# Two expert stages rewritten as units of two column tiles, in a two-layer diffusion backbone

## The reference, cut to what matters

```python
scores = sigmoid(t @ router_w); sel = scores + router_bias      # t: (T, 1024), T = 512 or 256
idx = top_8_of_64(sel, limited to the best 4 of 8 groups)
w = scores[idx] / sum(scores[idx]) * 2.5
for e in range(64):                                             # w_gate, w_up: 1024 x 256, w_down: 256 x 1024
    rows = tokens that chose e
    y[rows] += ((silu(t[rows] @ w_gate[e]) * (t[rows] @ w_up[e])) @ w_down[e]) * w[rows, e]
out = y + swiglu(t, shared_w_gate, shared_w_up, shared_w_down)
```

## Time and profile before

| | us |
|---|---|
| median of three executions | 2116.54 |
| the profiled execution | 2115.48 |
| its span, from the first to the last instruction | 2113.5 |
| TensorE busy | 1841.8 (87%) |
| VectorE busy | 1147.1 (54%) |
| ScalarE busy | 751.6 (36%) |
| GpSimd busy | 323.1 (15%) |
| layer 0's expert matmuls, first to last | 468.2 to 1153.2 |
| layer 1's expert matmuls, first to last down product | 1573.3 to 2091.2 |

### The profile page before, as it was taken

One profiled execution on the slowest core, in us unless ns is written; L12 is line 12 of the kernel. 1 busy time (PEld: TensorE's weight loads), 2 busy tenths in 40 slices (PEclk: granted clock), 3 DMA queues, 4 the chain that ended last, 5 costly groups with the idle time before them and its releaser, 6 DMA issues. The chain is left out here.

```text
span 2113.5 us, 32804 instructions
## 1 busy us (share of the span) xinstructions
PE 1841.8 (87%) x9706; PEld 1177.2 (56%) x9707; DVE 1147.1 (54%) x1988; ACT 751.6 (36%) x1200; POOL 323.1 (15%) x365
## 2 busy tenths in 40 slices
PE   2798989769999999999998679973769999999996
PEld 0677864436667766666665268311435555555553
DVE  1424643267777777777775655464333343343344
ACT  1214431126666665656553134772101111111111
POOL 1210000011112111222221070120001111111110
PEclk9999989789999999999999889985879999999998
DMA  6761043518899999999994853633449999999993
GB/s 263 250 241 41 1 147 129 195 50 301 345 364 359 353 352 359 371 364 357 351 354 181 345 131 102 214 118 140 159 166 414 420 419 416 413 419 415 415 418 131
DMA packets 127189, 580.28 MB, mean 275 GB/s; under 512 B 31347, under 2 KB 52457, under 8 KB 66849
## 3 DMA queue, kind: packets, MB, share of 16 engines
q1 hardware_dynamic: 94624, 500.76, 60.8%
q0 software_dynamic: 32368, 76.74, 10.1%
q10 hardware_dynamic: 144, 2.10, 0.3%
HBM read 587.79 MB, written 38.90 MB: 297 GB/s over the span
## 5 line engine op out<-in xcount | busy, mean ns | idle before, releaser
L1497 DVE TENSOR_TENSOR m_w_lo<-mods,m_w_hi 128x1024 fp32r<-128x1024 f32 x264 | 311.6, 1222 | 33.1 <-ACT m_w_hi L1416 30.7
L1416 ACT ACTIVATE m_w_hi<-mods 128x1024 fp32r<-128x1024 f32 x264 | 263.9, 1049 | 21.5 <-PEq L1008 11.9
L1694 PE MATMUL ps<-m_wgu,m_xT 128*64 128x256 f32 x2112 | 251.1, 385 | 4.3 <-DVE m_xT L1793 4.3
L1368 PE MATMUL ps<-m_w_hi,m_x_hi 128*128 128x512 f32 x528 | 245.3, 465 | 5.6 <-DVE m_x_lo L1489 5.6
L1352 PE MATMUL ps<-m_wd,m_hidT 128*128 128x512 f32 x528 | 248.1, 592 | 0.9 <-DVE h L1505 0.9
L1694 PEld LDWEIGHTS ps<-m_wgu,m_xT 128*64 128x64 f32 x2112 | 159.1, 138 | 98.1 <-issue 46.9
L1368 PE MATMUL ps<-m_w_lo,m_x_hi 128*128 128x512 f32 x528 | 208.2, 394 | 0.0
L1368 PE MATMUL ps<-m_w_hi,m_x_lo 128*128 128x512 f32 x528 | 207.0, 392 | 0.0
L1799 DVE TENSOR_TENSOR h<-h,ps 128x512 f32<-128x512 f32 x132 | 90.5, 686 | 124.5 <-PE ps L1683 123.5
L1352 PEld LDWEIGHTS ps<-m_wd,m_hidT 128*128 128x128 f32 x528 | 95.5, 191 | 70.8 <-issue 63.6
L1284 POOL DMA_INDIRECT h<-h_rows,m_gidx x69 | 79.7, 1156 | 350.6 <-DVE m_gidx L1481 345.8
(11 more groups left out here) (316 smaller groups left out, 3173.0 us busy)
## 6 DMA issues: line engine op xcount, KB each, us to landing
m_wd<-in_moe_w_down SPq DMA_DIRECT2D x132, 1024.0 KB, 9.0
mods<-in_moe_w_gate SPq DMA_DIRECT2D x66, 1024.0 KB
mods<-in_moe_w_up SPq DMA_DIRECT2D x66, 1024.0 KB
m_wgu<-in_moe_w_gate SPq DMA_DIRECT2D x66, 1024.0 KB
m_wgu<-in_moe_w_up SPq DMA_DIRECT2D x66, 1024.0 KB, 12.7
c_rows<-y_rows SPq DMA_DIRECT2D x8, 2048.0 KB, 15.4
mods<-in_ada_w POOLq DMA_DIRECT2D x11, 1024.0 KB, 6.4
mods<-in_ada_w SPq DMA_DIRECT2D x11, 1024.0 KB, 4.8
```

Source lines behind the costliest of these rows:

```text
L1368: last = pe.matmul(g.ps[0:S, GU, :].rearrange("p (a f) -> p a f", a=2), x[:, q, k, :], w[:, q, :, k, :], start=(k == 0 and n == 0), stop=( ...
L1416: act.activation(w_hi[:, q, :, k, :], wgu[:, q, :, k, :], ACT.Copy).then_inc(hi_s, 1)
L1497: dve.tensor_tensor(w_lo[:, q, :, k, :], wgu[:, q, :, k, :], w_hi[:, q, :, k, :].bitcast(F32), ALU.subtract).then_inc(lo_s, 1)
L1694: last = pe.matmul(g.ps[half[s], GU, a * FE:(a + 1) * FE], xT[:, k, half[s]], wgu[:, q, s, a, k, :], start=(k == 0), stop=(k == KD - 1))
```

## The change

Both expert phases are replaced by one, `unit_phase`, and both weight classes by `UnitWeights`. An expert's rows are cut into halves of up to 64 rows. Two halves of the same expert make a *twin* unit, and what is left over after that (one half at most for each expert) is joined with another expert's into a *pair* unit. A twin unit loads its expert's weights once and uses them on both column tiles; a pair unit loads two experts. `side` is 1 for a pair and 0 for a twin. Pairs stand at even positions and twins at odd ones as long as there are both. By the counts above, layer 0 has 20 pairs (one with an empty second half) and 26 twins, 46 units; layer 1 has 32 pairs (one with an empty second half) and one twin, 33 units.

The step of a unit is that of the pair phase before. In layer 0 the `put` and `add` parts are left out; the result is copied to `ysb` and scattered, as before. In layer 0 the down weights have two buffers (in `g.mods`), in layer 1 one.

The weights of the second half come from GpSimd's queue, by an indirect transfer with one row of 8 KB for each partition. Where there is no second expert, the indices are out of bounds and nothing is moved. `routes.second` holds the indices; VectorE copies a unit's column to `gu_row` and `down_row` in each step. The first loads wait until the owners of the units are known (`known`), since the order of the experts now comes from the routing. The route phase computes the order in a longer chain of small VectorE operations, with TensorE's shared gate and up products placed around it. The calls of `recycle_semaphores` move ahead of `combine_phase`.

```diff
+HB = P // 2
+NU = 72
+SKIP = 65536.0
+def lead_of(layer):
+    return 2 if layer == 0 else 1
...
+class UnitWeights:
+    def __init__(self, g, sb, layer, routes, wd):
...
+        self.wgu = sb(tag + "wgu", [P, 2, 2, 2, KD, FE])
+        self.wd, self.depth = wd, wd.shape[1]
...
+    def gate(self, sp, e, q):
+        sp.dma_start(self.wgu[:, q, 0, 0, :, :], self.first_rows[0][bass.ds(e, 1)].rearrange("o p k f -> p (o k) f")).then_inc(self.gate_in[q], 16)
...
+    def _second(self, pool, dst, n, row, landed):
+        rows = self.second_rows[n]
+        pool.indirect_dma_start(dst, None, rows, bass.IndirectOffsetOnAxis(ap=row[:, 0:1], axis=0),
+                                bounds_check=rows.shape[0] - 1, oob_is_err=False).then_inc(landed, 16)
+    def gate2(self, pool, q):
+        self._second(pool, self.wgu[:, q, 1, 0, :, :].rearrange("p k f -> p (k f)"), 0, self.gu_row[q], self.gate2_in[q])
...
     def prefetch(self, sp):
-        for q in range(2):
-            for s in range(2):
-                self.gate(sp, 2 * q + s, q, s)
...
+        for u in range(2):
+            e = self.owner(sp, u, 0)
+            self.gate(sp, e, u)
+            self.up(sp, e, u)
+            if u == 0:
+                self.down(sp, e, u)
+    def prefetch2(self, pool):
+        for u in range(2):
+            pool.wait_ge(self.gu_row_s, u + 1)
+            self.gate2(pool, u)
+            self.up2(pool, u)
...
 def route_phase(g, layer, tiles, routes, weights):
...
                 sp.wait_ge(g.h_stored, 16 * g.h_stores)
+                sp.wait_ge(known, 3)
                 weights.prefetch(sp)
+            @block.gpsimd
+            def _(pool):
+                weights.prefetch2(pool)
...
+                shared_gate_up(0)
                 pe.wait_ge(masks, 1)
...
+                pe.wait_ge(parts_s, 1)
+                for n in range(2):
+                    pe.matmul(g.ps[:, RANKS, n * (E + 1):(n + 1) * (E + 1)], parts[:, n:n + 1].to_broadcast([E, P]), g.field("before_e", E),
+                              start=True, stop=True)
...
+                shared_gate_up(1)
+                pe.wait_ge(at_s, 1)
+                pe.wait_ge(number_s, 1)
+                pe.matmul(g.ps[:, OWN, 0:3 * NU], number[:, 0:1].to_broadcast([E, P]), at[:].rearrange("e s u -> e (s u)"),
+                          start=True, stop=True).then_inc(owners, 1)
+                for t in range(2, tiles):
+                    shared_gate_up(t)
...
-def expert_phase(g, layer, tiles, routes, weights):
-def expert_pair_phase(g, layer, tiles, routes, weights, total):
+def unit_phase(g, layer, tiles, routes, weights, total=None):
...
+    half = (slice(HB, P), slice(0, HB))
...
             def _(sp):
+                def load(i, q):
+                    e = weights.owner(sp, i, 0)
+                    sp.wait_ge(gate_done, i - 1)
+                    sp.sem_inc(issue, 1)
+                    weights.gate(sp, e, q)
+                    sp.wait_ge(up_done, i - 1)
+                    sp.sem_inc(issue, 1)
+                    weights.up(sp, e, q)
+                def load_down(i, d):
+                    e = weights.owner(sp, i, 0)
+                    sp.wait_ge(y_done, i - depth + 1)
+                    sp.sem_inc(issue, 1)
+                    weights.down(sp, e, d)
...
             def _(pool):
...
+                def step(i, q, r):
+                    pool.wait_ge(weights.gu_row_s, i + 3)
+                    pool.sem_inc(issue, 1)
+                    weights.gate2(pool, q)
+                    weights.up2(pool, q)
+                    gather(i + 2)
+                    pool.wait_ge(y_done, i + 1)
+                    pool.sem_inc(issue, 1)
+                    if depth == 1:
+                        weights.down2(pool, 1 - q, 0)
+                    else:
+                        pool.wait_ge(weights.down_row_s, i + 3)
+                        pool.sem_inc(issue, 1)
+                        weights.down2(pool, q, q)
+                    if total is None:
+                        scatter(i, q)
...
             def _(pe):
...
+                def project(q, r, side, a, loaded, loaded2, done, inside=None):
+                    pe.wait_ge(loaded[q], 16 * r + 16)
+                    pe.wait_ge(loaded2[q], 16 * r + 16)
...
                         for s in range(2):
-                            last = pe.matmul(g.ps[half[s], GU, a * FE:(a + 1) * FE], xT[:, k, half[s]], wgu[:, q, s, a, k, :],
+                            w = wgu[:, q, 0, a, k, :] if s == 0 else wgu[:, q, bass.ds(side, 1), a, k, :].rearrange("p o f -> p (o f)")
+                            last = pe.matmul(g.ps[half[s], GU, a * FE:(a + 1) * FE], xT[:, k, half[s]], w,
                                              start=(k == 0), stop=(k == KD - 1))
...
                 def step(i, q, r):
+                    side = pe.value_load(routes.side[0:1, bass.ds(i, 1)], min_val=0, max_val=1)
...
+                    if total is None or first(i):
+                        project(q, r, side, 1, weights.up_in, weights.up2_in, up_done)
                     else:
                         put(i - 1, 0, TB)
+                        project(q, r, side, 1, weights.up_in, weights.up2_in, up_done, inside=lambda: put(i - 1, 1, TB))
                     turn_tokens(i + 1)
...
             def _(dve):
...
                     dve.scalar_tensor_tensor(hid[:], act_g[:], meta[:, bass.ds(i, 1), GAIN], g.ps[:, GU, FE:2 * FE], ALU.mult, ALU.mult).then_inc(hid_s, 1)
+                    dve.tensor_scalar(weights.gu_row[q][:], routes.second[:, bass.ds(i + 2, 1)], 0.0, None, ALU.add).then_inc(weights.gu_row_s, 1)
                     tokens(i + 1)
...
-                expert_phase(g, 0, TILES, routes, weights)
+                unit_phase(g, 0, TILES, routes, weights)
+            g.recycle_semaphores()
             combine_phase(g, 0, TILES)
...
-                expert_pair_phase(g, 1, LAT_TILES, routes, weights, total)
+                unit_phase(g, 1, LAT_TILES, routes, weights, total)
```

More of the change, by code:

```diff
@@ L961, in route_phase @@
     tag = f"r{layer}"
-    E, S = EXPERTS, slots_of(tiles)
-    full = tiles * P // S
+    E = EXPERTS
+    full = tiles * P // HB
+    twin = full // 2
     with ExitStack() as st:
@@ L1148, in _ @@
                 dve.tensor_copy(chosen_bf[:], chosen[:]).then_inc(masks, 1)
-                for t in range(tiles):
+                dve.wait_ge(pos_done, 1)
+                chain.link(dve.tensor_copy(filled[:], g.ps[0:E, OWN, COUNT:COUNT + 1]))
+                chain.link(dve.tensor_scalar(over[:], g.field("iota_b", E)[:, 0:full], float(HB), filled[:, 0:1], ALU.mult, ALU.is_lt))
+                chain.done(dve.tensor_reduce(parts[:, 0:1], over[:, 0::2], AX.X, ALU.add))
+                chain.link(dve.tensor_reduce(parts[:, 1:2], over[:, 1::2], AX.X, ALU.add))
@@ L1150, in _ @@
+                chain.link(dve.tensor_tensor(firsts[:, 0:1], firsts[:, 1:2], all_two, ALU.add))
+                chain.link(dve.tensor_scalar(routes.count[:], firsts[0:1, 0:1], float(-1 - lead_of(layer)), None, ALU.add))
+                for t in range(1, tiles):
                     hidden(t)
-                dve.wait_ge(pos_done, 1)
-                for j in range(1, full):
-                    chain.link(dve.tensor_scalar(over[:, j:j + 1], g.ps[0:E, POS, COUNT:COUNT + 1], float(S * j), None, ALU.is_gt))
@@ new lines, in _ @@
+                for j in range(2, twin):
+                    chain.link(dve.scalar_tensor_tensor(turn, pos, float(P * j), turn, ALU.is_ge, ALU.add))
+                chain.link(dve.tensor_tensor(turn, turn, per_expert(two), ALU.add))
+                chain.link(dve.tensor_scalar(turn, turn, 1.0, firsts[:, 1:2], ALU.add, ALU.min))
+                chain.link(dve.tensor_tensor(base, per_expert(single[:]), turn, ALU.subtract))
+                chain.link(dve.tensor_tensor(base, base, alone, ALU.mult))
@@ L1653, in slots @@
                 def slots(i):
-                    experts = [owner(pe, 2 * i + s) for s in range(2)]
+                    experts = [weights.owner(pe, i, s) for s in range(2)]
                     pe.wait_ge(onehot_s, i + 1)
-                    if not peeled(i):
+                    if not first(i):
                         pe.wait_ge(idx_s, i)
```

769 lines of the change are left out of this document (265 added, 504 removed).

## The result

The changed kernel takes 2206.39 us (median of four runs, 2204.97 to 2218.56), the kernel before 2116.38 beside it: a ratio of 1.0443, with a 95% interval of 1.0403 to 1.0483. The forecast was 2084, so the sign was wrong, and so was the range. The profiled execution has a span of 2204.8 us, 91.3 more than before.

A forecast was written before the change was run, and what follows sets the result against it. TensorE was taken to bind layer 0, TensorE and DMA level in layer 1. The sum 2115.5 − 43 + 1 + 1 + 8 = 2082.5 us, 2084 against the median; the forecast's own range 2065 to 2105, overall 2045 to 2128.

The forecast's parts named there:

- TensorE's 13.2 us for a unit: Layer 0: TensorE needs 13.2 us a unit, 607 us for 46 units, as the stage's floor against 684.9.
- The DMA's 28.6 us for a period: Layer 0: a pair and a twin need 28.6 us of DMA, TensorE 26.4, so DMA binds; stage 642 us.
- the stage's −43: Layer 0's expert stage: 642 us, 43 less than before.
- The gather comes late in layer 0: Rival, chance 0.14: gather behind gate2 and up2 lands 4 to 5 us late; stage 690 to 730, time 2132 to 2172.
- q1 has nothing queued in parts of the period: Layer 0: argument against the late-gather rival, since gate and up loads are issued early.
- The two covers in layer 1: Layer 1 step: gather lands near 19 us, wanted at 24.3; down2 near 24.5, wanted at 27.5; both hold.
- +8: Layer 1's stage: 33 steps 0.3 us longer each, 10 us, less 2 for six loads spared.
- Two full queues are slower than one: Rival, chance 0.14: layer 1 falls to 383 GB/s, 17.1 us a step, 46 us instead of 8; time 2122.
- Where layer 0 starts: Route phase before layer 0: longer ordering against gathered rows needing no splitting, net +1 us.
- +6: Layer 0's route phase: VectorE's added links, longer slot chain and TensorE's wait for ranks push the tail 6 us.
- Between the layers +1: Layer 1's route phase: taken as 1 us longer.
- Register work: Register addresses of second-half matmuls: counted as hidden; as a rival, chance 0.08, 30 us in layer 1, 2114 or less.

The follow-up runs named there:

- the rows decoupled: Two buffers of gathered rows, gather ordered one unit earlier, in layer 0 or both layers; alone in layer 0 of the changed kernel 2107.74 us, in both 2113.94 us.
- two buffers alone: Changed kernel with two buffers of gathered rows and the gather one unit earlier in layer 0, nothing else: 2107.74 us, ratio 0.996.
- q0 at a third of the DMA: Kernel with two buffers of gathered rows in both layers, layer 1's down2 alone moved to SyncE's queue: 2066.78 us.
- the filler: Changed kernel with five 128x512 matmuls into an unused bank ahead of the wait for rows, every second unit of layer 0: 2222.59 us.

## Why the prediction was wrong, by its own steps

**TensorE's 13.2 us for a unit: right.** 13.12 in the rows above, 13.1 to 13.2 in the last six units, and 610.1 for the stage when nothing has to be loaded for the second half.

**The DMA's 28.6 us for a period, and 642 for layer 0: too dear, and not what was at work.** With the rows decoupled the period is 27.3 us and the stage 622 to 624 in four kernels. The error is 19 us, in the kernel's favour. Its likely source, which no run separates, is the price of a row, which came from a stage in which TensorE bound. What failed lies elsewhere: the sum took a period as the longer of the DMA's 28.6 and TensorE's 26.4 us, as if the two overlapped in full, and put no wait between them. The period measured is 32.8, and the stage's −43 was +42.1.

**"The gather comes late in layer 0" was a rival with 0.14, and is what happened.** Its mechanism is shown: two buffers alone took layer 0 from 727.0 to 622.2. Its working had the times of the issues right (gate2 9.4 us after the gate product, the gather 12.1; forecast 10.3 and 12.3), had found no slack, and had named the period that decides, 30.8; 32.8 came, and a stage of 727 inside its 690 to 730. The step that failed is the weighing: "q1 has nothing queued in parts of the period". In the earlier trace rows the loads stand against a TensorE that is never late; here q1 had 37 to 48% of the DMA engines' time between gate2's issue and the turning, and q0 46 to 62%. The forecast of that rival, q1 with every second packet, had it about right. The Trainium skill, DMA: Bandwidth & Descriptors, Queues, rings and completion order, says that each engine goes round the queues packet by packet, and the trace agrees in so far as both queues moved bytes all through the gather's wait. The same section says that a transfer's semaphore comes only behind that engine's earlier writes, of any queue; no run here separates this from the wait in the queue.

**The two covers in layer 1 failed too, and the same queue is in it.** The prediction had the gather land "near 19" and down2 "near 24.5" in a step. The issues came as said: the gather 1913.76 − 1898.74 = 15.0 us after the gate product, down2 1.1 us after the next. But the gather of 1898.29 took 9.5 us after its issue where I allowed 4, and down2 some 14 where I allowed 8. In q0 gate2, up2, gather and down2 follow each other, 3.6 MB, and from 1895 to 1914 q0 moved 3.59 MB in 19 us, 48.6% of the DMA engines' time. I had spent the whole DMA's rate on a queue that gets half. Down2, whose buffer is single, seems to count most: with rows decoupled layer 1 stayed at 551, with down2 moved to the other queue it came to 520, with all three to 517.5. So +8 was 34.9; how much of it is lateness and how much is rate stays open, as the next step says.

**"Two full queues are slower than one" (0.14) gave nearly the right time for layer 1 (17.1 us a step; 16.75 came) and is not refuted.** It doesn't hold for any two queues: with q0 at a third of the DMA the rate is 400 GB/s at a share of 0.98, or 408 at a full share, against 413 with one queue. But with q0 at half of it the changed kernel moves 387 at 0.98, or 395 at a full share, and the kernel with two buffers in both layers 388 at 0.98. Some 4% are lost while the engines are busy, and 3% while they aren't; a step is 7% longer than before. With half the bytes from ScalarE's queue it was 407 at 1.00 and a stage of 529. No run moves down2 and keeps q0's part at half, so none separates the late down2 from the rate, or says why the rate falls.

**Where layer 0 starts: +1 was +8.6.** Ten kernels with this route phase started at 472.9 to 476.8, so up to 4 of it are scatter. With the second shared tile ahead of the slot chain three kernels started at 471.0 to 474.0: in the mean 2.6 us earlier, though the two ranges touch. So probably some 3 us were the order on VectorE, whose cost I had named (+6) and then set off against the work that was gone. The rest is open. First loads were in, as said, and cost nothing. Between the layers +1 was +6.1, of which I have no cause; it was 423.6 to 431.6 in all kernels with the change's route phase in layer 1, 426.3 here and 420.2 before.

**Register work: nothing,** as forecast.

**The clock: not in the prediction.** It fell from 1.00 to a mean of 0.92 in layer 0, and down products behind a wait took up to 6.3 us instead of 3.8, since part of them ran at the lower of the two levels, 1.2 GHz (granted clock 0.50 from 861.1 to 862.0, right behind the longest wait). TensorE was busy 630.4 us in the stage against 580.9 for the same work with two buffers, so its products took 49.5 us longer, 2.5 a period. The low level comes behind the waits and goes with them. Whether it costs time of its own beyond them is not shown: the filler put more work in than it took waiting away. The Trainium skill, TensorE: Matmul & The Clock Gate, Terms, gives time at the lower level a penalty in proportion; for a mean of 0.92 over 700 us that is an estimate of 56 us, near the 49.5, but it doesn't say how much of it reaches the stage's time.

The sum by the terms as measured: 2115.5 + 8.6 + 42.1 + 6.1 + 34.9 − 0.3 = 2206.9, against 2206.6 of the profiled execution. The saving that the change was capable of was there, 684.9 − 622.2 = 63 us in layer 0. It was lost to one buffer of 4 KB a partition: two buffers in layer 0, with nothing else, give 2107.74 and no loss against the kernel before.

## What to carry to other kernels

When loads move to a queue that also carries a small, urgent transfer, price that transfer at what stands ahead of it in its queue, at the share of the DMA that the queue gets while the others are full (here 41 to 62%, 169 to 231 GB/s), and not at its own size. Look for the thing that has one buffer: its slack is one step less the issue, and a full DMA eats it first; reordering the queue moved the wait from one single-buffered tile to another, and in layer 0 a second buffer removed it. Where both TensorE and the DMA have gaps, look for a buffer that each hands to the other before counting on the rate of either. And time a filler before reading anything from it: if it takes longer than the waits that it fills, it becomes the load.

## What was unexpected

- Issuing the urgent transfer first bought 33 us in layer 0 and cost 52 in layer 1; holding everything back until it had landed made layer 0 50 to 80 us slower. The backlog of the step before decides.
- Some 105 us of useless matmuls in layer 0 made the stage 14 us longer than 727.0, within its scatter: they took the place of waits and of products at the low clock.
- Layer 0 of the changed kernel took 724 to 743 us in four executions of the same code, while with two buffers four kernels agree within 2 us.
